# Storing the experts' results with an indexed GpSimd DMA that leaves empty places out, in a one-core decoder step

## The chip, the core and the metric

The kernel is one program on one core of a Trainium2 chip. The metric is the device time of one execution in microseconds, the median over the runs of the same kernel. A profiled execution gives the trace; its times count from the first instruction of the program, and its span ends with the last.

The engines are named as in the profile: PE (TensorE; PEld its weight loads), DVE (VectorE), ACT (ScalarE), POOL (GpSimd) and SP (SyncE, which only issues DMAs here). A q behind a name (POOLq, SPq) is that engine's sequencer, which issues and waits.

## The reference, cut to what matters

One layer of a decoder runs for 1024 prompt tokens and 64 sample tokens. After attention, a gated MLP and their merge, every token goes to two of 32 experts:

```
order = jnp.argsort(flat_e)
counts = jnp.zeros((N_EXPERTS,), jnp.int32).at[flat_e].add(1)
...
slot_tok = jnp.full((P,), T, jnp.int32).at[dest].set(flat_tok[order])
...
def run_block(args):
    xi, e = args
    return (jax.nn.silu(xi @ w_g[e]) * (xi @ w_u[e])) @ w_d[e]
yb = lax.map(run_block, (xb, block_e)).reshape(P, D)
out = jnp.zeros((T + 1, D), jnp.float32).at[slot_tok].add(yb.astype(jnp.float32) * slot_w[:, None])
```

So tokens are sorted by expert into blocks of 128 places, a block is run through its expert's three matrices (1024x512, 1024x512, 512x1024, fp32), and each token adds its two results, weighted. Places that no token fills have no part in the output. After that come a gate, a projection, norms and the output rows.

## The kernel before

The program is a row of stages, each a block in which all five engines run their own hand-written order; a stage ends with a barrier of all engines (in the trace each engine shows a DRAIN and an EVENT_SEMAPHORE there, on the line that opens the stage's block). Around the change they are: prompt attention (line 785), sample attention, merge, output projection, routing and experts in one block (line 2256), overflow (line 2449), and the final stage (line 2594).

**The experts.** The 32 experts are ranked by load. The 16 largest get a unit of 128 places each, the 16 smallest share 8 units, 64 places each: `NUNIT` is 24. Beyond them stand `NOVER` = 20 spare blocks for tokens of an expert that overflows its unit, so the table of results `c.y_d` (named moe_out) has `SLOTS` = 44 x 128 rows of 1024 floats, 4 KB a row. Per unit u, GpSimd gathers the token rows from moe_in in four indexed DMAs of a quarter row each (`gather_rows`), DVE lays them out (`lay_x`, which frees the gather's buffer and signals `xt_set`), PE makes gate, up and down products, DVE multiplies (`multiply`), and ACT copies the result out of PSUM into one of two buffers `Y` (`keep_y`, signal `y_done`) and stores all its 128 rows in moe_out with one DMA on its own queue, 512 KB. On PE the order is gate of u+1, down of u, up of u+1. SP streams the weights, 96 loads of 2 MB through nine slots, each issued when PE has left its slot.

**GpSimd's order in the experts' stage** is: the gathers of units 0 and 1, a small norm, then for u from 2 to 23 a wait for `xt_set` (u-1 units laid out) and the gather of u.

**The table's spare blocks** have to hold zeros or anything finite only where something reads them; they are cleared in the prompt attention. There GpSimd, in step with PE's gate products (semaphore `gate_mm`, one for each of 48 pieces), issues five DMAs of a 2 KB row of zeros repeated, 2 MB each. SP loads the gates' weights in the same stage, 1 MB for every two pieces, when `gate_mm` says that PE has begun the block before; the wait values 8q+6 of the clears are even, so that a clear is issued in the same microsecond or so as a load. PE needs that load when it comes to the first piece two pieces on (line 915).

**The end.** When the experts' block is left, the overflow stage loads the number of overflow blocks on each engine and steps over its loops (there is no overflow in these inputs), and the final stage begins: GpSimd waits for all stores of results and gathers two rows of moe_out per token, 128 tokens at a time (line 2622), while PE keeps itself busy with idle products (line 154), then turns the rows and makes the last gate products (lines 2674 and 2689).

The routing that the changed lines belong to runs on DVE as a chain of small operations, nearly each waiting for the one before (`do`, `tt`); `c.idx` holds for each place of a block the sum over its tokens of token number minus 4096, thus 0 where no token is. `block_at` is 128 times the block's number.

Of the kernel before, what the change touches and what calls it, by code (L numbers as in the profile page):

```python
# [15 lines left out]
I32 = mybir.dt.int32  # L16
U32 = mybir.dt.uint32
ALU = mybir.AluOpType
# [3 lines left out]
P = 128  # L22
D = 1024
# [16 lines left out]
PLE = 256  # L40
# [9 lines left out]
STRIPS = 4  # L50
SW = P // STRIPS
QW = D // STRIPS
NOWHERE = 4096
# [4 lines left out]
W_AT = HT_AT + TOK * KD  # L58
# [26 lines left out]
def bcast(ap, n):  # L85

    return ap.unsqueeze(2).to_broadcast([ap.shape[0], ap.shape[1], n])
# [43 lines left out]
def view(c, at, *dims):  # L131
    n = int(np.prod(dims))
    v = c.arena[:, at:at + n]
    if len(dims) == 1:
        return v
    names = "abcd"[:len(dims)]
    return v.rearrange(f"p ({' '.join(names)}) -> p {' '.join(names)}",
                       **{k: d for k, d in zip(names, dims)})
# [595 lines left out]
def stage_prompt_attention(nc, c):  # L734
# [50 lines left out]
    with nc.Block() as block:  # L785
        @block.sync
        def _(sp):
# [44 lines left out]
            c.load_keys(sp, 0, 2)  # L832
            sp.wait_ge(c.blank_out, 16 * BLANKS)

        @block.gpsimd
        def _(pool):
            pool.wait_ge(c.out_rows, 16 * 7)
            g_ = nc.gpsimd
            g_.memset(zeros, 0.0).then_inc(blank, 1)
            g_.memset(c.CN, 0.0).then_inc(c.cleared, 1)  # L840
            g_.memset(c.NOUGHT, 0.0).then_inc(c.cleared, 1)
            g_.memset(AT[:, NP], 0.0).then_inc(c.cleared, 1)
            pool.wait_ge(c.cn_in, 16 * H)
            for b in range(DB):
                g_.tensor_tensor(c.NBN[:, b, :], c.CN, c.new_mask[:, NS - b * DT:2 * NS - b * DT],
                                 ALU.add).then_inc(c.nbn_done, 1)
            pool.wait_ge(blank, 1)
            spare = c.y_d[NUNIT * P:].rearrange("(p n) (a d) -> p (n a) d", p=P, a=2)
            each = 2 * NOVER // BLANKS
            for q in range(BLANKS):  # L850
                pool.wait_ge(gate_mm, 8 * q + 6)
                pool.dma_start(spare[:, q * each:(q + 1) * each, :],
                               zeros.unsqueeze(1).to_broadcast([P, each, D // 2])).then_inc(c.blank_out, 16)
            pool.wait_ge(c.pages_in, 16)
            c.first_values = [c.page_numbers(pool, 0, ch) for ch in range(NCH)]
# [204 lines left out]
                    keep_out(m - 2)  # L1060


BLANKS = 5
CH = 4
NCH = PAGES // CH
NTI = P // 32
# [770 lines left out]
NUNIT = NSINGLE + NPAIRED  # L1837
GROUP = 5
NOVER = 20
SLOTS = (NUNIT + NOVER) * P  # L1840
HALF = P // 2
UNITS = []
# [6 lines left out]
LATE_AT = T_AT - 7 * WBLK  # L1849
# [63 lines left out]
def stage_route(nc, c):  # L1913
# [16 lines left out]
    iota, bonus, step_no, SEL, lane, block_at, tok, strip_no, step8 = route_tables(c)  # L1930
# [20 lines left out]
    xg_in = c.xg_in = [c.kept_sem(f"xg_in{j}") for j in range(2)]  # L1951
    c.g_strips = view(c, LATE_AT - NUNIT * STRIPS - QW, QW)
    c.quarter_i = view(c, LATE_AT - NUNIT * STRIPS, STRIPS, NUNIT).bitcast(I32)
    quarters_of_rows = c.h2_d.rearrange("t (s n) -> (t s) n", s=STRIPS)

    def gather_rows(g, u):
# [147 lines left out]
    def route_dve(dve):  # L2104
        v = nc.vector
# [11 lines left out]
        def tt(out, a, b, op):  # L2117
            do(v.tensor_tensor(out, a, b, op))
# [8 lines left out]

        dve.wait_ge(c.logit_mm, NT)
        dve.wait_ge(c.aux, NAUX)
        tt(LG, c.bank[6][:, 0:NT * K].rearrange("p (t k) -> p t k", k=K), bcast(c.stat[:, 2, :], K), ALU.mult)  # L2130
        tt(LG, LG, over_tiles(c.b_route[:], K), ALU.add)
        dve.sem_inc(logits_read, 1)
# [73 lines left out]
        for ch in range(NCHUNK):  # L2206
            if ch >= 2:
                dve.wait_ge(idx_mm, ch - 1)
            n = ch * LANES
# [8 lines left out]
                        strip_no, ALU.mult, ALU.add).then_inc(c.quarter_done, 1)  # L2218


        BY_RANK = GT
        tt(BY_RANK[0:1], lane[0:1, 0:NE].unsqueeze(2).to_broadcast([1, NE, NE]),
           rank[0:1].unsqueeze(1).to_broadcast([1, NE, NE]), ALU.is_equal)
# [14 lines left out]
def stage_moe(nc, c):  # L2238
# [4 lines left out]
    Y = view(c, MOE_AT + 6 * D, 2, D)  # L2243
# [4 lines left out]
    y_out = c.y_out = [c.kept_sem(f"y_out{j}") for j in range(2)]  # L2248
# [3 lines left out]
    down_mm, y_done = c.kept_sem("down_mm"), c.sem("y_done")  # L2252
# [3 lines left out]
    with nc.Block() as block:  # L2256
# [24 lines left out]
        @block.gpsimd  # L2281
        def _(pool):
            c.route["pool"](pool)
            g = nc.gpsimd
            for u in range(2, NUNIT):
                pool.wait_ge(xt_set, u - 1)
                c.gather_rows(g, u)

        @block.tensor
        def _(pe):  # L2290
# [63 lines left out]
        @block.scalar  # L2354
        def _(act):
            c.route["act"](act)
            s = nc.scalar

            def silu(u):
                act.wait_ge(gate_mm, u + 1)  # L2360
                if u >= 1:
                    act.wait_ge(act_done, CELLS * u)
                s.activation(SG, gate_ps[:, :], ACT.Silu).then_inc(silu_done, 1)  # L2363

            def keep_y(u):
                b = UNITS[u][0]
                act.wait_ge(down_mm, u + 1)
                if u >= 2:
                    act.wait_ge(y_out[u % 2], 16 * (u // 2))
                s.activation(Y[:, u % 2, :], y_ps, ACT.Copy).then_inc(y_done, 1)  # L2370
                act.wait_ge(y_done, u + 1)
                act.dma_start(c.y_d[b * P:(b + 1) * P, :], Y[:, u % 2, :]).then_inc(y_out[u % 2], 16)

            silu(0)
            for u in range(NUNIT):
                if u + 1 < NUNIT:
                    silu(u + 1)
                keep_y(u)
# [524 lines left out]
```

## Time and profile before

| | us |
|---|---|
| median of 3 runs | 1859.94 |
| lowest and highest run | 1856.11, 1860.59 |
| the profiled execution | 1858.34 |
| its span in the trace | 1856.7 |
| PE busy in the span | 1765.6 (95%) |
| DVE, ACT, POOL busy | 751.6, 317.8, 271.6 |
| DMA moved | 432.38 MB, mean 233 GB/s |

The span is 1.6 us shorter than the time of its execution. PE's busy time is the length of its work as the trace models it. What counts for a change is which wait ends last at its place: the page's shares are averages over stages, of which the prompt attention (344 to 706 us) leaves the DMA engines half idle and the experts' stage (1133 to 1700 us) keeps them busy throughout. "DMA share" in a row by windows is the mean busy share of the 16 DMA engines. Landing is the time from a DMA's issue to the semaphore that tells of its end.

### The profile page before, as it was taken

Reading aid. Unit: us, or ns where it says so; the run is one execution under the profiler, and the core shown is the slowest. Engines: PE = TensorE matmul, PEld = TensorE weight load, DVE = VectorE, ACT = ScalarE, POOL = GpSimd, SP = SyncE. Lnnn points to the kernel's source line nnn. Section 1 sums busy time; section 2 is a strip of 40 time slices with the busy share of each in tenths; the row PEclk is TensorE's granted clock in tenths of the full one; section 3 lists DMA queues with packets and bytes.
Section 4 is the critical chain, followed back from the end, with each engine's and each line's share of the span. In section 5 each row is a group of like instructions: output and inputs, shape, how many; then the busy total and the mean of one; then the engine's idle time right before and its main releaser. Section 6 shows DMA issues by size and latency. Waiting matters only on the chain. (4 is left out here: it accounts for less than half of the span.)

```text
span 1856.7 us, 23215 instructions
## 1 busy us (share of the span) xinstructions
PE 1765.6 (95%) x8503; PEld 894.0 (48%) x8503; DVE 751.6 (40%) x1539; ACT 317.8 (17%) x552; POOL 271.6 (15%) x390
## 2 busy tenths in 40 slices
PE   7999999899999998979999998999999999998997
PEld 4564554556566664544455444443333333433443
DVE  4201104433334354555322226444444444443665
ACT  2000001222222233322110113200000000000122
POOL 1000004200000002332300000421111122100330
PEclk9999999999999999999999999899999999998999
DMA  8012110344344638999747425699999999998541
GB/s 288 6 19 87 49 52 1 107 139 162 117 162 142 219 100 293 355 378 330 261 170 284 162 82 229 224 344 424 423 425 424 425 423 424 421 429 320 199 153 62
DMA packets 137027, 432.38 MB, mean 233 GB/s; under 512 B 26581, under 2 KB 65194, under 8 KB 124626
## 3 DMA queue, kind: packets, MB, share of 16 engines
q1 hardware_dynamic: 101026, 337.16, 47.7%
q0 software_dynamic: 20288, 62.98, 9.4%
q10 hardware_dynamic: 15600, 30.75, 4.4%
q8 instruction: 68, 1.11, 0.2%
q14 instruction: 45, 0.37, 0.1%
HBM read 378.99 MB, written 55.51 MB: 234 GB/s over the span
## 5 line engine op out<-in xcount | busy, mean ns | idle before, releaser
L2308 PE MATMUL psum<-arena 128*128 128x512 f32 (+1 forms) x1024 | 337.1, 595 | 0.0
L915 PE MATMUL psum<-arena 128*128 128x384 f32 (+1 forms) x768 | 253.9, 476 | 4.2 <-ACT arena L946 4.1
L2410 DVE TENSOR_TENSOR arena<-arena,psum 32x128 f32<-32x128 f32 x384 | 143.4, 373 | 267.2 <-PE psum L2308 256.0
L2308 PEld LDWEIGHTS psum<-arena 128*128 128x128 f32 (+1 forms) x1024 | 131.6, 163 | 203.0 <-issue 203.0
L2339 PE MATMUL psum<-arena 128*64 128x512 f32 (+1 forms) x512 | 170.4, 596 | 10.0 <-issue 6.0
L915 PEld LDWEIGHTS psum<-arena 128*128 128x128 f32 x768 | 139.8, 191 | 77.8 <-issue 6.0
L1959 POOL DMA_INDIRECT arena<-moe_in,arena x96 | 98.5, 1026 | 385.3 <-DVE arena L2392 322.4
L2339 PEld LDWEIGHTS psum<-arena 128*64 128x64 f32 (+1 forms) x512 | 68.5, 163 | 111.9 <-issue 111.9
L1764 PE MATMUL psum<-arena 128*128 128x512 f32 x256 | 114.7, 604 | 1.6 <-PEq L1539 1.6
L2689 PE MATMUL psum<-arena 128*128 128x512 f32 x256 | 111.4, 592 | 1.4 <-DVE arena L2721 1.4
L330 PE MATMUL psum<-arena 128*128 128x512 f32 x256 | 111.8, 593 | 0.7 <-DMA arena<-in_w_in 0.7
L1195 POOL DMA_DIRECT2D arena<-in_cache_v x112 | 60.1, 537 | 121.3 <-PE psum L1299 114.4
L1764 PEld LDWEIGHTS psum<-arena 128*128 128x128 f32 x256 | 48.2, 192 | 59.0 <-issue 59.0
L2689 PEld LDWEIGHTS psum<-arena 128*128 128x128 f32 x256 | 47.9, 190 | 58.5 <-issue 58.5
L1230 PE MATMUL psum<-arena 128*128 128x512 f32 x160 | 73.4, 601 | 2.6 <-DVE arena L1440 2.6
L330 PEld LDWEIGHTS psum<-arena 128*128 128x128 f32 x256 | 47.9, 190 | 57.9 <-issue 57.0
L953 ACT ACTIVATE arena<-arena 128x128 f32<-128x128 f32 (+7 forms) x64 | 49.1, 768 | 144.1 <-DVE arena L1017 80.4
L1426 DVE STREAM_TRANSPOSE arena<-arena 128x2048 f32<-128x2048 f32 x27 | 61.8, 2300 | 21.9 <-DMA arena<-in_cache_k 21.9
L2363 ACT ACTIVATE arena<-psum 128x512 f32<-128x512 f32 x24 | 14.3, 597 | 301.4 <-PE psum L2308 301.4
L390 PE MATMUL psum<-arena 128*128 128x384 f32 (+1 forms) x192 | 58.7, 469 | 1.6 <-DVE arena L536 1.6
L355 PE MATMUL psum<-arena 128*128 128x384 f32 (+1 forms) x192 | 58.8, 469 | 0.0
L644 PE MATMUL psum<-arena 128*128 128x512 f32 x128 | 56.8, 598 | 1.7 <-PEq L225 0.9
(298 smaller groups left out, 1846.6 us busy)
## 6 DMA issues: line engine op xcount, KB each, us to landing
arena<-in_w_exp_gate SPq DMA_DIRECT2D x32, 2048.0 KB, 22.1
arena<-in_w_exp_up SPq DMA_DIRECT2D x32, 2048.0 KB, 18.9
arena<-in_w_exp_down SPq DMA_DIRECT2D x32, 2048.0 KB, 21.4
arena<-in_cache_v POOLq DMA_DIRECT2D x128, 256.0 KB, 9.4
arena<-in_cache_k SPq DMA_DIRECT2D x124, 256.0 KB, 8.6
arena<-in_w_in SPq DMA_DIRECT2D x24, 1024.0 KB, 6.2
moe_out<-arena ACTq DMA_DIRECT2D x24, 512.0 KB, 10.4
arena<-in_w_in SPq DMA_DIRECT2D x5, 2048.0 KB, 20.1
```

The source lines that it names most:

```text
L330: last = mm(c.bank[4 + r % 3][:, :], hidden_tile(HT, t)[:, k, :], W[:, n + 1, k, :], start=(k == 0), stop=(k == KD - 1))
L355: last = mm(c.bank[n % 4][:, 0:CUTS[sec + 1] - CUTS[sec]], W[:, 0, k, j * P:(j + 1) * P], HT[sec][:, k, :], start=(k == 0), stop=(k == KD ...
L915: done = mm(c.bank[7][:, 0:b - a], WG[blk % 2][:, k, q * P:(q + 1) * P], HT[p // NCOL][:, k, :], start=(k == 0), stop=(k == KD - 1))
L1195: pool.dma_start(VC[:, ch, g, :], c.cache_v[bass.ds(numbers[ch][g] * P, P), :]).then_inc(v_in[ch], 16)
L1230: last = mm(c.bank[7][:, :], UP[col % 2][:, n, k, :], src[:, 4 * half:4 * half + 4, k, :], start=(k == 0), stop=(k == KF - 1))
L1426: v.transpose(keys, keys).then_inc(turned[b % 2], 1)
L1764: last = mm(c.bank[2 * (t % 2) + half][:, :], MT[:, k, t * P:(t + 1) * P], WO[:, k, half * 512:half * 512 + 512], start=(k == 0), stop=(k ...
L1959: g.indirect_dma_start(out=XG[:, u % 2, q, :], out_offset=None, in_=quarters_of_rows, in_offset=bass.IndirectOffsetOnAxis(ap=c.quarter_i[: ...
L2308: last = mm(out[rows_, :], XT[:, u % 2, k, rows_], c.ring_tile(LOAD[kind, u, r])[:, k, :], start=(k == 0), stop=(k == KD - 1))
L2339: last = mm(y_ps[rows_, cols], ACT_T[:, u % 2, k, rows_], c.ring_tile(LOAD["down", u, r])[:, k, cols], start=(k == 0), stop=(k == KF - 1))
L2410: v.tensor_tensor(ACT_T[SW * s:SW * s + SW, u % 2, :, SW * q:SW * q + SW], SG[r, cols].rearrange("p (d k) -> p k d", k=KF), up_ps[r, cols] ...
L2689: last = mm(gate_ps[t % 2][:, half * 512:half * 512 + 512], XT[:, t % 2, k, :], c.wpg[half][:, k, :], start=(k == 0), stop=(k == KD - 1))
```

## The change

Results are no longer stored by ACT. GpSimd stores unit u's 128 rows with an indexed DMA whose index per row is the place in moe_out, or `SLOTS` more than that where no token fills the place; a bounds check drops such rows. Since those rows of moe_out are then not written, the whole table is cleared in the prompt attention instead of its 20 spare blocks, in four DMAs instead of five. DVE works out the indices with one operation at the start of the routing and four at its end. GpSimd's order gets the store of unit u-3 behind the gather of u, and the last three stores follow the last gather.

```
-            spare = c.y_d[NUNIT * P:].rearrange("(p n) (a d) -> p (n a) d", p=P, a=2)
-            each = 2 * NOVER // BLANKS
+            spare = c.y_d.rearrange("(p n) (a d) -> p (n a) d", p=P, a=2)
+            each = 2 * SLOTS // P // BLANKS
...
-BLANKS = 5
+BLANKS = 4
...
+        place_in_block = c.stat[:, 3, 0:1]
+        do(v.tensor_scalar(place_in_block, tok[:, 0:1], float(NOWHERE), None, ALU.add))
...
+        do(v.tensor_scalar(row_f, c.idx[:, 0:NUNIT], 0.0, float(SLOTS), ALU.is_equal, ALU.mult))
+        tt(row_f, row_f, block_at[:, 0:NUNIT], ALU.add)
+        do(v.tensor_scalar(row_f, row_f, place_in_block, None, ALU.add))
+        v.tensor_copy(c.row_i, row_f).then_inc(c.rows_done, 1)
...
+            def scatter(u):
+                b = UNITS[u][0]
+                pool.wait_ge(y_done, u + 1)
+                g.indirect_dma_start(out=c.y_d, out_offset=bass.IndirectOffsetOnAxis(ap=c.row_i[:, b:b + 1], axis=0),
+                                     in_=Y[:, u % 2, :], in_offset=None,
+                                     bounds_check=SLOTS - 1, oob_is_err=False).then_inc(y_out[u % 2], 16)
+
+            pool.wait_ge(c.rows_done, 1)
             for u in range(2, NUNIT):
                 pool.wait_ge(xt_set, u - 1)
                 c.gather_rows(g, u)
+                if u >= 3:
+                    scatter(u - 3)
+            for u in range(NUNIT - 3, NUNIT):
+                scatter(u)
...
             def keep_y(u):
-                b = UNITS[u][0]
                 act.wait_ge(down_mm, u + 1)
                 if u >= 2:
                     act.wait_ge(y_out[u % 2], 16 * (u // 2))
                 s.activation(Y[:, u % 2, :], y_ps, ACT.Copy).then_inc(y_done, 1)
-                act.wait_ge(y_done, u + 1)
-                act.dma_start(c.y_d[b * P:(b + 1) * P, :], Y[:, u % 2, :]).then_inc(y_out[u % 2], 16)
```

GpSimd in the experts' stage, from the block's start to its end, in the kernel before; moe_in is where token rows are gathered from, and the last row but one leaves the block:

```order
L1634 UNCONDITIONAL_BRANCH
L2281 UNCONDITIONAL_BRANCH
L1959 DMA arena<-moe_in,arena 128x256 x8
L2008 TENSOR_SCALAR arena<-arena 128x9
L2010 TENSOR_TENSOR arena<-arena,neghalf 128x9
L1959 DMA arena<-moe_in,arena 128x256 x88
L2256 UNCONDITIONAL_BRANCH
L2467 UNCONDITIONAL_BRANCH
```

Every gather is done with when the block still has some 70 us to go. The end of the same list in the changed kernel, where line 1963 is the gather and 2300 the store:

```order
L1963 DMA arena<-moe_in,arena 128x256 x4
L2300 DMA moe_out<-arena 5632x1024
L1963 DMA arena<-moe_in,arena 128x256 x4
L2300 DMA moe_out<-arena 5632x1024
L1963 DMA arena<-moe_in,arena 128x256 x4
L2300 DMA moe_out<-arena 5632x1024 x4
L2267 UNCONDITIONAL_BRANCH
L2488 UNCONDITIONAL_BRANCH
```

A store stands between every two gathers, and four stores follow the last gather; the last of them waits for the last result of the stage and is GpSimd's last instruction in the block. ACT at the same end, in the kernel before (2370 copies a result out of PSUM, 2372 stores it):

```order
L2370 ACTIVATE arena<-psum 128x1024
L2372 DMA moe_out<-arena 128x1024
L2370 ACTIVATE arena<-psum 128x1024
L2372 DMA moe_out<-arena 128x1024
L2256 UNCONDITIONAL_BRANCH
```

In the changed kernel the copies stand alone, and the branch out of the block follows the last copy.

GpSimd in the prompt attention, the difference at the clears:

```order
 L845 TENSOR_TENSOR arena<-arena,new_mask 128x64 x8
-L852 DMA moe_out<-arena 128x8x512 x5
+L852 DMA moe_out<-arena 128x22x512 x4
 L1084 TENSOR_LOAD arena
```

The clears stand where they stood; each is 22 half rows a partition instead of 8, and the fifth is gone.

## Rows read from the trace of the kernel before

**Rows 1.** Waits of PE, 1195 to 1710 us: total, times, longest
```profile
PE psum L154 <- PEq L2449: 6.8, 1, 6.8
PE psum L2339 <- issue: 6.0, 15, 0.4
```
**Rows 2.** Windows: length, busy by engine (x count), PE clock, DMA share, GB/s
```profile
1400.00:1500.00 100.00, 98.36 (x292) 39.48 (x290) 42.22 (x84) 7.51 (x9) 19.95 (x20) 1.00 1.01 423
```
**Rows 3.** Waits of PE, 380 to 700 us
```profile
PE psum L915 <- ACT arena L946: 0.9, 3, 0.3
```
**Rows 4.** Timeline of POOL and of SPq: start, length, engine line
```profile
451.44 0.89 POOL L852 DMA_DIRECT2D moe_out<-arena  x1 [62.95 <-PE psum L915]
...
387.79 0.43 SPq L790 DMA_DIRECT2D arena<-in_w_in  x1
...
452.05 0.43 SPq L790 DMA_DIRECT2D arena<-in_w_in  x1
...
572.53 0.43 SPq L790 DMA_DIRECT2D arena<-in_w_in  x1
```
**Rows 5.** Landing of the gate weights' loads issued at 452.05 and 466.19
```profile
DMA to landing us min/median/max: 11.7/11.7/11.7
...
DMA to landing us min/median/max: 5.6/5.6/5.6
```
**Rows 6.** DMA queues in 454 to 458 us: packets, MB, share
```profile
q0 software_dynamic: 306, 1.25, 79.5%
q1 hardware_dynamic: 294, 0.30, 21.3%
```
**Rows 7.** Timeline of PE where it turns to the freshly loaded weights
```profile
404.27 2.75 PE L915 MATMUL psum<-arena 128*128 128x384 f32 x8
...
465.95 2.82 PE L915 MATMUL psum<-arena 128*128 128x384 f32 x8 [0.30 <-ACT arena L946]
...
589.01 2.32 PE L915 MATMUL psum<-arena 128*128 128x320 f32 x8
```
**Rows 8.** Timeline of DVE in the routing
```profile
1141.26 0.17 DVE L2150 TENSOR_SCALAR arena<-arena 128x9 f32<-128x9 f32 x1
...
1174.32 2.02 DVE L2392 TENSOR_TENSOR arena<-arena 128x1024 f32<-128x1024 f32 x1 [1.15 <-DMA arena<-moe_in,arena]
```
**Rows 9.** Timeline of POOL, ACT and DVE in the experts' loop
```profile
1292.93 1.00 POOL L1959 DMA_INDIRECT arena<-moe_in,arena  x1 [16.68 <-DVE arena L2392]
...
1297.50 1.02 ACT L2370 ACTIVATE arena<-psum 128x1024 f32<-128x1024 f32 x1 [6.93 <-PE psum L2339]
...
1332.99 2.00 DVE L2392 TENSOR_TENSOR arena<-arena 128x1024 f32<-128x1024 f32 x1
```
**Rows 10.** Landing of 22 of ACT's 24 stores, 1200 to 1690 us
```profile
DMA to landing us min/median/max: 8.9/10.5/11.1
```
**Rows 11.** Timeline of ACT and POOL: the last result, the last gather's last part
```profile
1698.74 1.02 ACT L2370 ACTIVATE arena<-psum 128x1024 f32<-128x1024 f32 x1 [7.27 <-PE psum L2339]
...
1618.80 0.99 POOL L1959 DMA_INDIRECT arena<-moe_in,arena  x1 [0.30 <-issue]
```
**Rows 12.** End of the experts' block, by its line: duration ns, start
```profile
L2256 POOLq EVENT_SEMAPHORE  x2: 17/17/17, 1700.4 to 1700.4; - x2
L2256 POOLq DRAIN  x1: 16844/16844/16844, 1616.2 to 1616.2; - x1
...
L2256 ACTq DRAIN  x1: 153/153/153, 1700.2 to 1700.2; - x1
```
**Rows 13.** End of the sample attention's block, by its line
```profile
L1161 POOLq DRAIN  x1: 14646/14646/14646, 909.4 to 909.4; - x1
```
**Rows 14.** Landing of POOL's last two loads before it (issued 908.8, 909.4)
```profile
DMA to landing us min/median/max: 12.4/12.9/13.4
```
**Rows 15.** Landing of the final stage's first gather (issued at 1706.2)
```profile
DMA to landing us min/median/max: 4.6/4.6/4.6
```
**Rows 16.** Timeline of PE at the start of the final stage
```profile
1705.51 11.69 PE L154 MATMUL psum<-before 128*128 128x512 f32 x20 [6.81 <-PEq L2449]
```

More of the change, by code:

```diff
@@ L1953, in stage_route @@
     c.quarter_i = view(c, LATE_AT - NUNIT * STRIPS, STRIPS, NUNIT).bitcast(I32)
+    row_at = LATE_AT - NUNIT * STRIPS - QW - NUNIT
+    assert row_at >= W_AT + 8 * D + (PLE // P) * D
+    row_f, c.row_i = view(c, row_at, NUNIT), view(c, row_at, NUNIT).bitcast(I32)
+    c.rows_done = c.kept_sem("rows_done")
     quarters_of_rows = c.h2_d.rearrange("t (s n) -> (t s) n", s=STRIPS)
```

## The prediction

> **What bounds the kernel now.** I read the waits of PE first, then the DMA share by windows, then the ends of the blocks. The reader is to see that PE is the bound at every place that the change touches but one. In the experts' loop PE's own waits are 6.0 us in 15 pieces, and the rest of the list is shorter [rows 1]. The DMA engines are busy throughout that loop, at 423 GB/s [rows 2], yet no wait of PE is put down to a weight load: the DMA keeps exactly the pace of PE. In the prompt attention PE waits 0.9 us in all [rows 3]. The one place where PE stands is the passage from the experts to the final stage, 6.8 us [rows 1, 16]: the last result is copied at 1698.74, the barrier opens at 1700.4 [rows 11, 12], and PE restarts at 1705.51. Whatever holds that barrier holds all engines.
>
> **Fewer rows stored.** 1088 tokens times 2 are 2176 filled places of 3072, so 896 rows of 4 KB, 3.67 MB, are no longer written. At 423 GB/s that is 8.7 us of DMA time [rows 2]. It is worth nothing where PE isn't waiting for a DMA; it only lets the weights land earlier. I take 0. If the DMA were the bound it would give the 8.7 us.
>
> **The store behind the gathers.** In the loop the gather of unit v+4 starts at 1292.93, when DVE has laid out v+2; v's result is copied at 1297.50 to 1298.5 [rows 9]. In the new order the store of v stands ahead of that gather and waits for the copy. So the gather starts at 1298.6 plus 1.3 for the store's own issue (one row of 1.0 and a gap of 0.3), 1299.9, that is 7.0 us later. Queued behind the waiting store are only gathers; who waits for them is DVE's layout at 1332.99. From the first part's issue to a DRAIN that outlasts a gather the trace has 18.1 us (1614.90 to 1633.0, the first part being 3.9 ahead of the row at 1618.80) [rows 11, 12]. Add the whole landing of a store ahead of it, 11.1 us at most [rows 10]: 1299.9 + 18.1 + 11.1 = 1329.1, still 3.9 us before DVE asks. Cost 0; and when this cover is gone, each unit would lose what the gather is late. The two buffers of results are reused after two units, some 43 us, against a landing of 11. ACT is freed of 24 issues, but waits for PE anyway.
>
> **Indices.** One small DVE operation is 0.17 us, 0.2 with its gap [rows 8]. The one at the head of the routing lies in the chain that PE waits for: 0.2 us. The four at the end take 0.8 us and fall in the 1.15 us in which DVE waits for the first gather [rows 8]: 0. GpSimd's wait for them stands ahead of the gather of unit 2, which starts 20 us later.
>
> **The clears.** A clear is issued at 451.44, a load of gate weights at 452.05 [rows 4]. That load landed after 11.7 us, one without a clear beside it after 5.6 [rows 5]. While both run, the queues take turns, 306 packets of the clear and 294 of the load in 4 us [rows 6]; 1.25 MB over 306 is 4 KB a packet, 0.30 over 294 is 1 KB. So the load's 1024 packets need 1024 / 73.5 = 13.9 us if the clear lasts as long. The old one had 512 packets and ended in the middle; the new one has 1408 (5.77 MB), so it does last. A landing has start and end beside the packets. By the share in [rows 6] 294 packets of the load occupy 21.3% of 4 us, 0.85, so its 1024 take at least 3.0 of the quiet load's 5.6, and up to 2.6 are left; gaps between packets make that less, I take 1.6. So the load lands 15.5 us after its issue, at 467.5, and PE, which turned to it at 465.95 [rows 7], waits 1.6. Counted from the 11.7 instead, the second 512 packets now take 7.0 us in turns where alone they took 1.5, which gives 17.2: PE then waits 3.3 there, and 0.7 each at the first and the fourth clear, where 15.5 is just in time (403.3 against 404.27, 588.0 against 589.01) [rows 4, 7] and the third has more room: 4.7. I take 1.5, near the first count, since the 4 us of [rows 6] hold only full turns and no quiet time; the bounds are 0.5 and 4.7. The far end is a clear that passes whole before the load: 2 MB cost 6.1 us, 5.77 MB then 16.8, so landing after 22.4, which is 5.9 + 8.5 + 5 + 5.9 = 25 us over the four. [rows 6] speak against it. The fifth clear's absence frees nobody. Sum for the clears: 1.5.
>
> **The last store, and the block's end.** This is the main term. Before, POOL had long been drained when the stage ended, and the barrier at 1700.4 came right behind ACT's short DRAIN of 153 ns [rows 12]: ACT's store was still under way. GpSimd's DRAINs are of another kind. At the experts' end it lasted 16.8 us, from 1616.2 to 1633.0, though the last DMA's issue was over at 1619.8 [rows 11, 12]. At the sample attention's end it lasted until 924.05 [rows 13], and the last DMA, issued at 909.4, landed 13.4 us later, at 922.8 [rows 14]. So it ended 1.2 us after that landing. For the gather, whose landing the trace doesn't give, a landing like the stores' 10.5 would be 1629.3 [rows 10], and the DRAIN ended 3.7 after it. I read: a DRAIN on GpSimd waits until its DMAs have landed, and then 1.2 to 3.7 us. The new last store goes out at 1699.85 behind the copy [rows 11]. Beside little other traffic an indexed DMA of the same 512 KB lands after 4.6 us [rows 15]: 1704.45. With 1.2, the row in which DVE was idle as it is here, the DRAIN ends at 1705.65 and the barrier opens at 1705.7 instead of 1700.4: 5.3 us. With 3.7 it is 7.8. Nothing covers it, since PE and all others stand at this barrier, and the walk over the overflow stage, the idle products and the first gather all follow it unchanged [rows 16]. What was late before, the products at line 154, is late by the same amount.
>
> The Trainium skill (DMA: Bandwidth & Descriptors, Anatomy of one DMA) gives a DMA issued by GpSimd as 2.0 us plus its bytes over 436 GB/s, an estimate of 3.2 us for this store. The measured landing of 4.6 us for the same size is longer and decides; by the page's figure the term would be 3.9 instead of 5.3, and the sum 5.6.
>
> **Sum.** 5.3 + 1.5 + 0.2 + 0 = 7.0 us. The profiled execution of 1858.34 becomes 1865.3; it lay 1.6 below the median of 1859.94, which becomes 1866.9, slower by 0.38%. With the bounds of the two terms, 5.3 to 7.8 and 0.5 to 4.7, it is 1865.9 to 1872.6, both upper ends at once being unlikely; a last unit of small experts with few filled rows could land 1 us sooner, 1864.9.
>
> **Rivals.** (a) *GpSimd's DRAIN waits only for descriptors.* Then its last issue of 1.0 us moves the barrier by 0.6 us, and the final stage's own wait for the store (1704.45) is over before its first gather at 1706.2. Sum 0.6 + 1.7 = 2.3: 1862.2, no measurable change. For it: other DRAINs take a fraction of a microsecond; against it: the two long ones. (b) *The DRAIN takes a fixed time behind the last DMA.* Both rows fit this nearly better: 14.2 us after the issue at 1618.80 and 14.6 after 909.4. Then the barrier opens at 1699.85 + 14.4 = 1714.2, 13.9 us late; with 1.7 more 1875.5. Against it only that I know no reason for such a wait. (c) *The clears pass whole, or the gathers come late*: 25 us and more in place of 1.5, some 1890, for the reasons above unlikely. (d) *The DMA is the hidden bound of the experts' loop*, the relief of 8.7 us is real, and (a) holds: 1859.94 - 8.7 + 2.3 = 1853.5, faster. It decides only if PE waits for weights, and [rows 1] have no such wait. (e) That the empty rows are written after all would change the DMA's work and not the time, since nothing hangs on it; the forecast stands in that case.
>
> The Trainium skill (SBUF — State Buffer, two separate sides) says that GpSimd cannot write DMA descriptors while DVE holds their shared port. By it a store issued during DVE's layout waits for that to end; at the last store DVE is idle, so it would add nothing to the main term.
>
> **How the numbers follow.** Chances: forecast 0.62, (a) 0.18, (b) 0.10, (c) 0.06, (d) 0.04. A measurement of this kernel can tell about 0.3%, 5.6 us, from no change; the line is 1865.5. The forecast's case stretches from 1864.9 to about 1871 and noise of the median carries some of it below the line; I put 0.47 above and 0.15 within. Slower: 0.47 + 0.10 + 0.06 = 0.63; same: 0.15 + 0.18 = 0.33; faster 0.04. The range is to take in the forecast and (a), with a microsecond or two of spread of the median: 1860.5 to 1872.0, leaving out (b), (c) and (d), 0.20.
>
> **What would show it.** In the changed kernel's trace: at the experts' block's end a DRAIN on POOLq that begins near 1700 and ends about 1706, the barrier just behind it, and ACT's DRAIN some 5 us before it; PE's wait at line 154 near 12 us instead of 6.8; a wait of PE on in_w_in near 466 of 1 to 2 us and none or little at the other clears; no wait of DVE on moe_in within the loop beyond the first two units. Rival (a) shows the barrier at 1701; (b) shows it at 1714; (c) shows long waits on in_w_in or moe_in; (d) shows an experts' loop with a shorter cycle. The forecast is wrong if the barrier moves by less than 4 us, or if PE's loop changes its pace at all.

## The result, and the profile after

Over 20 runs of each on the same chip the changed kernel has a median of 1861.64 us (1856.88 to 1869.28) and the kernel before 1855.66 (1850.06 to 1861.39). The ratio is 1.003, with a 95% interval of 1.0019 to 1.0041: slower by about 5.6 us (the two medians lie 6.0 us apart; the ratio is an estimate over all runs and not the quotient of the medians). Two further comparisons on other occasions gave 1.0019 [1.0009, 1.0029] and 1.0020 [1.0008, 1.0032], 3.5 and 3.7 us. The forecast was slower by 7.0 us, to 1866.9. So the sign held, and the time lies in the stated range, but the size did not hold. The absolute time came out 5.3 us below the forecast, and 4.3 us of that is luck of the start: the median of three runs from which the forecast counted (1859.94) stands that much above the median of twenty. The time also lies below 1865.5, the prediction's own line between slower and the same, and next to the 1862.2 of its rival (a), whose mechanism the trace refutes below.

The profiled execution took 1864.14 us, its span 1862.5. The first view is the waits of PE at the end of the experts' stage in the changed kernel (engine, line, what it waited for; total, times, longest), to be read against [rows 1]:

```profile
PE psum L154 <- PEq L2470: 10.3, 1, 10.3
PE psum L2710 <- DVE arena L2742: 1.4, 1, 1.4
PE psum L2363 <- ACT arena L2393: 1.2, 1, 1.2
PE psum L2363 <- DVE arena L2436: 0.4, 1, 0.4
```

The wait at line 154 was 6.8 us and is 10.3. The 1.4, the 1.2 and the 0.4 are in the kernel before too, word for word but for the line numbers. Over the whole loop, 1195 to 1710 us, PE's waits of the changed kernel are these:

```profile
PE psum L2363 <- issue: 6.0, 15, 0.4
PE psum L2363 <- DVE arena L2436: 2.8, 7, 0.4
PE psum L2363 <- ACT arena L2393: 1.2, 1, 1.2
```

The first row equals its counterpart in [rows 1] to the last digit: the loop's pace has not changed. The end of the experts' block by its line (duration in ns, then the start), the answer to [rows 12]:

```profile
L2267 POOLq EVENT_SEMAPHORE  x2: 17/17/17, 1706.6 to 1706.7; - x2
...
L2267 ACTq DRAIN  x1: 1052/1052/1052, 1701.0 to 1701.0; - x1
L2267 POOLq DRAIN  x1: 4002/4002/4002, 1702.6 to 1702.6; - x1
```

GpSimd's DRAIN starts behind its last store instead of 84 us before the end, it ends at 1706.6, and the barrier opens there. ACT's DRAIN of 1.05 us covers the last copy and is over at 1702.0, 4.6 us before the barrier. The timelines of ACT, POOL and PE at this place (start, length; in brackets the idle time before and its releaser), the answer to [rows 11, 16]:

```profile
1700.98 1.02 ACT L2393 ACTIVATE arena<-psum 128x1024 f32<-128x1024 f32 x1 [7.27 <-PE psum L2363]
...
1702.80 0.97 POOL L2300 DMA_INDIRECT moe_out<-arena  x1 [7.33 <-ACT arena L2393]
...
1711.20 1.19 PE L154 MATMUL psum<-before 128*128 128x512 f32 x1 [10.26 <-PEq L2470]
```

The last copy ends at 1702.00, the store is issued 0.80 later, and it landed after 3.2 us, at 1706.0:

```profile
DMA to landing us min/median/max: 3.2/3.2/3.2
```

The DRAIN ends 0.6 us behind that landing. So from the end of the last copy to the open barrier the changed kernel takes 0.8 + 3.2 + 0.6 = 4.6 to 4.7 us, where the kernel before took 0.67; from the barrier to PE's first product it takes 4.5, where the kernel before took 5.1. I call the whole, from the last copy's end to PE's first product at line 154, the **passage**: 5.75 us before, 9.20 after, so 3.45 more.

In the prompt attention PE has no wait on a weight load, as in [rows 3]:

```profile
PE psum L915 <- ACT arena L946: 0.9, 3, 0.3
PE psum L887 <- ACT arena L962: 0.3, 1, 0.3
```

In the experts' loop (timeline of POOL) the store stands ahead of the gathers as forecast, with the first gather at 1302.95 for a copy that ended at 1300.80:

```profile
1301.63 1.02 POOL L2300 DMA_INDIRECT moe_out<-arena  x1 [15.21 <-ACT arena L2393]
1302.95 1.02 POOL L1963 DMA_INDIRECT arena<-moe_in,arena  x1 [0.31 <-issue]
1304.28 1.01 POOL L1963 DMA_INDIRECT arena<-moe_in,arena  x1 [0.30 <-issue]
```

**A trap in comparing the two spans.** They differ by 5.8 us, and only 3.45 of it is the passage. Of the rest, 1.9 us lie ahead of the experts' stage. Windows of the merge and of the output projection (length, busy by engine, PE clock, DMA share, GB/s), first of the kernel before, then of the changed one:

```profile
928.00:987.00 59.00, 55.55 (x224) 36.37 (x224) 15.71 (x30) 7.96 (x5) 0.00 (x0) 1.00 0.36 134
987.00:1133.00 146.00, 139.77 (x522) 68.62 (x522) 36.40 (x66) 24.55 (x28) 8.81 (x30) 0.98 0.46 179
```
```profile
926.30:987.00 60.70, 57.25 (x224) 37.26 (x224) 15.79 (x30) 7.96 (x5) 0.00 (x0) 0.97 0.36 130
987.00:1135.00 148.00, 141.93 (x522) 69.75 (x522) 36.39 (x66) 24.55 (x28) 8.82 (x30) 0.96 0.46 176
```

The same 224 and 522 products take 1.7 and 2.2 us longer at a lower mean clock (1.00 and 0.98 against 0.97 and 0.96; it has two levels, 1.2 and 2.4 GHz, and the changed kernel's execution had 82.5 us at the lower one, the earlier one 65.5). Neither stage is touched by the change. In the thirteen traces of this study the experts' stage begins anywhere from 1127.1 (end_2mb) to 1136.4 (short_walk), and these two kernels are the same up to there. So single spans are not compared below; what is compared is the passage in a trace, and the ratio over many runs.

One stretch of a trace can be compared, since it starts behind all that varies there: from the end of the last copy to the program's last instruction. It is 156.9 us in the kernel before, and 160.5, 160.9 and 160.2 us in the three traces of the changed kernel, 3.3 to 3.9 us longer. So what the passage loses does reach the end of the program.

### The profile page after: what moved, and what is told of

It is laid out like the page before. It is cut to its first block and busy times, and to the rows that moved or that the text cites. A ratio compares the mean times of both kernels' runs of the same rounds, so it can differ in the third digit from the quotient of the medians.

```text
span 1862.5 us, 23244 instructions
## 1 busy us (share of the span) xinstructions
PE 1770.8 (95%) x8503; PEld 898.0 (48%) x8503; DVE 752.6 (40%) x1544; ACT 317.7 (17%) x552; POOL 300.4 (16%) x413
## 5 line engine op out<-in xcount | busy, mean ns | idle before, releaser
L1764 PE MATMUL psum<-arena 128*128 128x512 f32 x256 | 116.0, 610 | 1.6 <-PEq L1539 1.6
L2710 PE MATMUL psum<-arena 128*128 128x512 f32 x256 | 111.4, 593 | 1.4 <-DVE arena L2742 1.4
L330 PE MATMUL psum<-arena 128*128 128x512 f32 x256 | 112.0, 595 | 0.0
L2300 POOL DMA_INDIRECT moe_out<-arena x24 | 24.3, 1014 | 371.1 <-ACT arena L2393 371.1
L1230 PE MATMUL psum<-arena 128*128 128x512 f32 x160 | 73.4, 602 | 2.6 <-DVE arena L1440 2.6
## 6 DMA issues: line engine op xcount, KB each, us to landing
arena<-in_w_exp_up SPq DMA_DIRECT2D x32, 2048.0 KB, 18.1
arena<-in_w_exp_down SPq DMA_DIRECT2D x32, 2048.0 KB, 18.4
```

The costliest lines, as they stand in the source:

```text
L330: last = mm(c.bank[4 + r % 3][:, :], hidden_tile(HT, t)[:, k, :], W[:, n + 1, k, :], start=(k == 0), stop=(k == KD - 1))
L1230: last = mm(c.bank[7][:, :], UP[col % 2][:, n, k, :], src[:, 4 * half:4 * half + 4, k, :], start=(k == 0), stop=(k == KF - 1))
L1764: last = mm(c.bank[2 * (t % 2) + half][:, :], MT[:, k, t * P:(t + 1) * P], WO[:, k, half * 512:half * 512 + 512], start=(k == 0), stop=(k ...
L2710: last = mm(gate_ps[t % 2][:, half * 512:half * 512 + 512], XT[:, t % 2, k, :], c.wpg[half][:, k, :], start=(k == 0), stop=(k == KD - 1))
```

## The experiments

The theory after this profile: **the whole cost is GpSimd's late DRAIN, and the rest of the change is free.** Its rivals: the clears cost part of it; the loop pays something by the store ahead of the gathers; or it is not the landing that the DRAIN waits for. Ratios are to the kernel before on the same chip. In the table, c is the end of the last copy, "landing" that of GpSimd's last DMA from its issue, "tail" the time from the landing to the end of GpSimd's DRAIN, "walk" the time between the two barriers of the overflow stage (a barrier counted at its last row on POOLq). Landing and tail are left out where GpSimd's last DMA is long over.

| kernel | ratio, interval | c to barrier | landing | tail | walk | passage |
|---|---|---|---|---|---|---|
| before | 1 | 0.67 | | | 4.92 | 5.75 |
| changed | 1.0030 [1.0019, 1.0041] | 4.70 | 3.2 | 0.6 | 4.34 | 9.20 |
| changed_again | 1.0019 [1.0009, 1.0029] | 5.92 | 4.4 | 0.57 | 4.31 | 10.39 |
| changed_third | 1.0020 [1.0008, 1.0032] | 4.71 | 3.2 | 0.58 | 4.32 | 9.19 |
| last_by_act | 1.0013 [0.9998, 1.0027] | 1.06 | 7.9 | 0.54 | 4.69 | 5.91 |
| last_by_act_again | 0.9987 [0.9977, 0.9998] | 0.94 | 7.8 | 0.54 | 4.64 | 5.74 |
| clear_only | 1.0004 [0.9993, 1.0016] | 0.67 | | | 4.91 | 5.74 |
| all_rows | 1.0036 [1.0021, 1.0051] | 6.01 | 4.5 | 0.58 | 4.34 | 10.50 |
| plain_store | 1.0035 [1.0020, 1.0051] | 7.02 | 6.0 | 0.58 | 4.30 | 11.48 |
| end_small | 1.0048 [1.0034, 1.0062] | 9.01 | 4.3 | 4.3 | 4.27 | 13.44 |
| end_2mb | 1.0076 [1.0061, 1.0090] | 13.13 | 8.7 | 4.0 | 4.32 | 17.61 |
| short_walk | 0.9998 [0.9982, 1.0014] | 0.67 | | | 2.54 | 3.37 |
| last_two_short | 0.9988 [0.9977, 1.0000] | 0.68 | | | 2.45 | 3.28 |

**changed_again, changed_third.** The changed kernel, nothing edited.

> The changed kernel once more, so that the others of this call have it beside them on the same chip. Expected of both theories: 1.003 of the kernel before (1.002 to 1.004), the barrier at the experts' end about 4.7 us behind the end of the last result's copy, and PE's wait at line 154 near 10.3 us.

> The changed kernel, to stand beside the next two on the same chip. Expected: 1.002 to 1.003 of before, first idle product of the final stage 9 to 10.5 us behind the end of the last copy.

Both slower, by 0.19% and 0.20%. The passage is 4.6 and 3.4 us longer than before, the measured times 3.5 and 3.7. The store's landing was 3.2, 4.4 and 3.2 us, GpSimd's DRAIN 4.00, 5.22 and 4.01 us: with nothing edited, a landing 1.2 us longer made a DRAIN 1.2 us longer. Between issue and landing SP's queue, which loads ahead for the final stage, still moved 0.10, 0.20 and 0.07 MB beside the store. The store itself is smaller than the prediction took it: its queue shows 144 packets and 0.36 MB, which is 88 rows of 4 KB and 56 packets of 4 bytes; so 40 of its 128 places are empty (16 of the small packets are there without a dropped row too, as all_rows shows).

**last_by_act.** Only the last unit's rows are stored by ACT, as before the change; GpSimd's last store is then that of unit 22, issued some eight microseconds earlier. Every later wait for the stores is made to count ACT's too (not shown).

```
-            for u in range(NUNIT - 3, NUNIT):
+            for u in range(NUNIT - 3, NUNIT - 1):
                 scatter(u)
...
                 s.activation(Y[:, u % 2, :], y_ps, ACT.Copy).then_inc(y_done, 1)
+                if u == NUNIT - 1:
+                    b = UNITS[u][0]
+                    act.wait_ge(y_done, u + 1)
+                    act.dma_start(c.y_d[b * P:(b + 1) * P, :], Y[:, u % 2, :]).then_inc(c.y_last, 16)
```

> The changed kernel, but the last unit's 128 rows are stored whole by ACT, as before; the other 23 stay with GpSimd. Theory (the barrier waits for GpSimd's DRAIN, and that for the landing of its last DMA): the last store of GpSimd is now issued 8 us before the last copy, its DRAIN is over before ACT's, the barrier comes 0.7 us behind the last copy instead of 4.7, PE's wait at line 154 falls from 10.3 to 6.8 us, and the time is 3.5 us less than the changed kernel's, 1.001 of before. Rival (the index work or the full clear cost most of the 6 us): the passage may shorten, but the time stays near 1.003.

> The changed kernel with the last unit's rows stored by ACT, a second time, since the first left its ratio (1.0013) within both theories. Theory (the whole cost is the late barrier): the passage is 5.8 us as in the first trace, and the ratio 1.000 to 1.0005. Rival (some 2 us of the cost lie elsewhere): 1.001 to 1.002 again.

GpSimd's and ACT's DRAIN at the block's end of last_by_act:

```profile
L2268 POOLq EVENT_SEMAPHORE  x2: 17/17/17, 1697.1 to 1697.2; - x2
...
L2268 POOLq DRAIN  x1: 8650/8650/8650, 1688.4 to 1688.4; - x1
...
L2268 ACTq DRAIN  x1: 152/152/152, 1696.5 to 1696.5; - x1
```

GpSimd's DRAIN now spans 8.65 us, because its store needs 7.9 to land, but it ends at 1697.04, 0.9 us behind the last copy (1696.11), and the passage is back at 5.9 and 5.7 us. ACT's own store was issued at 1696.13 and landed 4.9 us later, at 1701.0, when the barrier had been open for 3.8 us: ACT's DRAIN of 152 ns waits for no landing. One store of 24 given back to ACT thus takes away the whole of the passage's growth, and everything else of the change is still in. From the last copy to the program's end these two traces have 156.9 us, as before the change. The ratios of the two occasions, 1.0013 and 0.9987, lie 0.26% apart for one and the same kernel, their intervals only touching. So one ratio with its interval promises more than it holds; half of that spread, 0.13%, is some 2.4 us. Their middle is 1.0000.

**clear_only.** The kernel before with the whole table cleared, in four DMAs; nothing else.

```
-            spare = c.y_d[NUNIT * P:].rearrange("(p n) (a d) -> p (n a) d", p=P, a=2)
-            each = 2 * NOVER // BLANKS
+            spare = c.y_d.rearrange("(p n) (a d) -> p (n a) d", p=P, a=2)
+            each = 2 * SLOTS // P // BLANKS
...
-BLANKS = 5
+BLANKS = 4
```

> The kernel before with one part of the change: the whole table of results is cleared, in four DMAs of 5.77 MB. Theory: in the trace of the changed kernel no wait of PE on the gate weights shows, so 1.000 of before, no wait on in_w_in, clears landing after 21 to 23 us. Rival (the clears cost part of the 6 us through PE or later stages): 1.001 to 1.002, with a wait of PE in the prompt attention.

1.0004, that is 0.7 us with an interval from -1.3 to 3.0, and PE's waits in the prompt attention are 0.9 and 0.3 us, as in the kernel before. The ratio alone would still allow the forecast's 1.5 us; it is the missing wait of PE that says that the clears cost nothing. Why, the changed kernel's trace tells. There the clears are issued at 385.70, 449.65, 508.70 and 570.11, each taking 1.35 to 1.46 us of POOL instead of 0.89 [rows 4], and the four loads beside them landed after 7.5, 10.8, 14.4 and 12.4 us, not after 15.5. The queues of the changed kernel in 452 to 454, 456 to 458 us and, around the third clear, 517 to 519 (packets, MB, share):

```profile
q1 hardware_dynamic: 333, 0.34, 83.5%
...
q0 software_dynamic: 162, 0.66, 80.5%
q1 hardware_dynamic: 161, 0.16, 22.9%
...
q0 software_dynamic: 162, 0.66, 80.5%
q1 hardware_dynamic: 162, 0.17, 23.3%
```

The turns are as [rows 6] gave them, packet by packet, 162 of the one to 162 of the other in 2 us. What the sum missed is when they begin. The clear's first packet stands at 454.5, 4.8 us after its issue; the old clear's at 453.3, 1.9 us after its own, before any packet of its load. In the changed kernel the load issued at 450.26 had by then passed some 500 of its 1024 packets alone. At the third clear the packets began after 3.0 us, the load had less of a start, and it landed after 14.4 us, near the 15.5 of the sum. That load was issued at 509.33 and landed at 523.7, and PE turned to it at 526.61.

The start varies, and its cause isn't known. The eight clears of 1408 packets in the changed kernel's trace and in clear_only's began 3.0 to 5.6 us after their issue; of the five of 512 packets in the kernel before four began after 1.8 to 1.9 us, but the first after 4.2.

**all_rows.** The changed kernel with indices that leave no row out.

```
-        do(v.tensor_scalar(row_f, c.idx[:, 0:NUNIT], 0.0, float(SLOTS), ALU.is_equal, ALU.mult))
+        do(v.tensor_scalar(row_f, c.idx[:, 0:NUNIT], 0.0, None, ALU.mult))
```

> The changed kernel, but the index leaves nothing out: empty places are written too (3072 rows instead of 2176). Theory (the rows left out are worth nothing in time, since PE never waits for a weight load): the same time as the changed kernel within 1 us, 1.002 of before; the weights' loads land after some 22 us again instead of 18; the very last store lands 0 to 1 us later, and the barrier with it. Rival (the DMA is a hidden bound and the relief is worth something): PE's cycle in the loop grows, some 8.7 us more in all.

**plain_store.** The changed kernel with GpSimd's stores in the same places but without indices, whole blocks of 128 rows.

```
-                g.indirect_dma_start(out=c.y_d, out_offset=bass.IndirectOffsetOnAxis(ap=c.row_i[:, b:b + 1], axis=0),
-                                     in_=Y[:, u % 2, :], in_offset=None,
-                                     bounds_check=SLOTS - 1, oob_is_err=False).then_inc(y_out[u % 2], 16)
+                pool.dma_start(c.y_d[b * P:(b + 1) * P, :], Y[:, u % 2, :]).then_inc(y_out[u % 2], 16)
```

> The changed kernel, but GpSimd stores each unit with a plain DMA of all 128 rows; the index is worked out and not used. It tells the indexed form from the plain one. Theory (DRAIN follows the landing, in 0.6 us): the last store lands after 4 to 5 us, the barrier comes 5 to 6 us behind the last copy, and the time is that of the changed kernel. Rival (behind a plain DMA of GpSimd the DRAIN takes 4.0 us more than the landing, as it did in the run with 2 MB at the end, behind an indexed store only 0.6): barrier 9 us behind the last copy, time 3.5 us above the changed kernel's.

1.0036 and 1.0035, 6.7 and 6.5 us slower; the passage grew by 4.75 and 5.7. The end of the block in plain_store:

```profile
L2267 POOLq EVENT_SEMAPHORE  x2: 17/17/17, 1707.8 to 1707.9; - x2
...
L2267 ACTq DRAIN  x1: 1052/1052/1052, 1699.8 to 1699.8; - x1
...
L2267 POOLq DRAIN  x1: 6624/6624/6624, 1701.1 to 1701.1; - x1
```

Neither the index nor the omission of rows makes the DRAIN wait: it is that the last DMA is GpSimd's. The plain store was issued sooner (0.30 us behind the copy instead of 0.80) and landed later, after 6.0 us against 4.5 for the same 128 rows in all_rows. But beside it SP's queue moved 0.73 MB, beside all_rows' store 0.33 and beside the changed kernel's 0.07 to 0.20. So whether the plain form is the slower one isn't shown; the landings rise with what SP still loads. The all_rows kernel writes 3.67 MB more than the changed one; whether leaving the rows out is worth anything by itself isn't separable: all_rows' ratio is above the changed kernel's three, and its interval overlaps all of theirs. Its last landing of 4.5 us is hardly longer than the changed kernel's 4.4. The expectation that the weights' loads would again need some 22 us with all rows written did not come true: their medians are 18.1 to 19.6 us.

**end_small, end_2mb.** The kernel before, all stores by ACT, with one additional DMA of GpSimd at the end of the block, into spare rows that nobody reads: 16 KB or 2 MB.

```
                 c.gather_rows(g, u)
+            pool.wait_ge(y_done, NUNIT)
+            pool.dma_start(c.y_d[NUNIT * P:NUNIT * P + P, 0:32], Y[:, 0, 0:32]).then_inc(c.end_out, 16)
```
```
                 c.gather_rows(g, u)
+            pool.wait_ge(y_done, NUNIT)
+            pool.dma_start(c.y_d[NUNIT * P:NUNIT * P + 4 * P, :].rearrange("(p n) d -> p n d", p=P), Y[:, 0, :].unsqueeze(1).to_broadcast([P, 4, D])).then_inc(c.end_out, 16)
```

> The kernel before, with one more DMA that GpSimd issues after the last result is copied: 16 KB into a spare block that nothing reads. Theory (0.6 us behind the landing): landing after about 2 us, barrier 2.7 to 3.5 us behind the last copy instead of 0.7, time 2 to 3 us more, 1.0013. Rival (4.0 us behind the landing of a plain DMA): barrier 6 to 7 us behind, time 5.5 us more, 1.003.

> The kernel before, with one more DMA that GpSimd issues after the last result is copied: 2 MB into spare rows of the table that nothing reads. It adds that work alone. Theory (DRAIN waits for the landing): the DMA lands after about 9.5 us, GpSimd's DRAIN ends 0.6 to 1.2 us later, the barrier comes 10.5 to 11.5 us behind the last copy instead of 0.7, the time is 10 us more, 1.0055. Rival (DRAIN lasts a fixed 4 us behind a DMA, whatever its size): barrier about 4.7 us behind the copy, time 3.5 to 4 us more, 1.002.

GpSimd's last DMA by its line, its landing, and the DRAIN behind it by the block's line (duration in ns, start), first in end_small, then in end_2mb:

```profile
L2290 POOL DMA_DIRECT2D moe_out<-arena x1: 594/594/594, 1696.9 to 1696.9; - x1
...
DMA to landing us min/median/max: 4.3/4.3/4.3
...
L2257 POOLq DRAIN  x1: 8616/8616/8616, 1696.9 to 1696.9; - x1
```
```profile
L2290 POOL DMA_DIRECT2D moe_out<-arena x1: 797/797/797, 1694.2 to 1694.2; - x1
...
DMA to landing us min/median/max: 8.7/8.7/8.7
...
L2257 POOLq DRAIN  x1: 12731/12731/12731, 1694.2 to 1694.2; - x1
```

The landing grew by 4.4 us from 16 KB to 2 MB, and the DRAIN by 4.1: the DRAIN follows the landing. That refutes both rivals of the prediction. By (a) the barrier should have opened a microsecond behind the copy, whatever the size; by (b) the DRAIN should have been 14 us long in each, and it was 8.6 and 12.7 here and 4.0 in the changed kernel. Nothing of the reference's work is changed in these two kernels, and 16 KB alone cost 8.9 us (1.0048), with 7.7 us of it in the passage. That is more than the changed kernel's 0.36 MB did, since the tail was 4.3 us here. Both expectations on record for end_small were too low: they put the landing near 2 us and the barrier at most 7 us behind the copy, and it was 9.0. From the last copy to the program's end the two traces have 164.2 and 168.0 us, against 156.9.

**short_walk, last_two_short.** The walk over the overflow stage, 20 spare blocks in groups of `GROUP`, each group's loop being stepped over by every engine. short_walk is the kernel before with one group; last_two_short is the changed kernel with one group, and with the last two units' rows stored by ACT.

```
-GROUP = 5
+GROUP = 20
```
```
-            for u in range(NUNIT - 3, NUNIT):
-                scatter(u)
+            scatter(NUNIT - 3)
...
+                if u >= NUNIT - 2:
+                    b = UNITS[u][0]
+                    act.wait_ge(y_done, u + 1)
+                    act.dma_start(c.y_d[b * P:(b + 1) * P, :], Y[:, u % 2, :]).then_inc(c.y_last, 16)
```

> The kernel before with the overflow stage's loops in one group of 20 blocks instead of four groups of 5. Without overflow every engine then steps over one group instead of four between the two barriers; where there is overflow it would run all 20 blocks. It asks whether a microsecond of this passage is a microsecond of the kernel. Theory: the stretch between the two barriers, 5.0 us, shrinks by 1.9 us (three turns of about 0.63 us on GpSimd), and the time with it, 0.999 of before. Rival (something else covers the passage, such as PE's idle products or the clock behind it): the stretch shrinks and the time stays at 1.000.

> The changed kernel with the last two units' rows stored by ACT, so that GpSimd's last DMA lands 15 us before the end, and with the overflow stage's loops in one group of 20 instead of four of 5. Theory: GpSimd's DRAIN is over before ACT's, the barrier 0.7 us behind the last copy, the first idle product 3.2 us behind it (5.6 in the kernel before), and the time 2.2 us below the kernel before, 0.9988, faster than both kernels. Rival (the passage is not worth its microseconds, or the store on GpSimd costs 2 us elsewhere): 1.000.

PE's wait at line 154, in short_walk and in last_two_short:

```profile
PE psum L154 <- PEq L2449: 4.4, 1, 4.4
```
```profile
PE psum L154 <- PEq L2474: 4.3, 1, 4.3
```

It fell by 2.4 and 2.5 us in the traces. The measured times moved by -0.4 us [-3.3, 2.6] and -2.2 us [-4.3, 0.0]: both hold the -2.4, but the first holds zero as well and the second ends there. In the traces the stretch from the last copy to the program's end did shrink, from 156.9 to 154.1 and 154.2 us. With an overflow, one group would run all 20 blocks where four could do with five, so this trades a rare case for the usual one.

**What was not tried.** The changed kernel with only the spare blocks cleared: places of moe_out that no store fills would stay unwritten. clear_only answers the same question from the other side.

**A version that beats both?** last_two_short and last_by_act_again stand at 0.9988 and 0.9987 of the kernel before, with intervals that end at 1.0000 and 0.9998, and below changed_third (1.0020) of the same chip. They beat the changed kernel. Against the kernel before they are at the edge of what these runs can tell, and the same kernel had given 1.0013 once.

## Why the prediction was right and wrong

**What bounds.** Right: PE's waits in the loop stayed at 6.0 us in 15 pieces, the DMA engines moved 421 GB/s in 1400 to 1500 us (423 before [rows 2]), and only the passage grew.

**The DRAIN.** Right in kind, and shown: GpSimd's DRAIN outlasts the landing of GpSimd's DMAs, and the barrier comes behind it (the three traces of the changed kernel, end_small, end_2mb), while ACT's doesn't (last_by_act). The term, 5.3 of the forecast's 7.0 us, was mis-sized. It was 5.3 for the barrier; measured are 4.0, 5.25 and 4.0 in three traces (c to barrier, less 0.67). In pieces: the store goes out 0.8 us behind the copy's end and not 0.1, so +0.7; it lands after 3.2 or 4.4 and not 4.6, so -1.4 or -0.2; the tail is 0.6 and not 1.2, so -0.6. The Trainium skill (DMA: Bandwidth & Descriptors, Anatomy of one DMA) gave 3.2 us for this landing by its figures; two of three traces have that value, the third has 4.4. But the 3.2 were worked out for 512 KB, and the store moved 0.36 MB, for which the page's sum is an estimate of 2.8; for all_rows' full 512 KB it is 3.2 against a measured 4.5, and end_small's 16 KB took 4.3 where it would be 2.0. So the agreement is in part chance. The tail was chance too: 1.2 us was chosen over 3.7 because DVE was idle in that row, and in end_small and end_2mb DVE is idle as well and the tails are 4.3 and 4.0.

**From the barrier to PE.** Wrong: it was said to be unchanged. With four groups in the overflow stage the walk between the two barriers was 4.3 us where GpSimd came last, and 4.6 to 4.9 where it didn't. So of the 4.0 to 5.25 PE saw 3.4 to 4.6, and its wait at line 154 became 10.3 us where the prediction's list of signs had about 12. Every late GpSimd in the table has this walk of 4.3; the cause isn't known, and no run tests it.

**The clears.** Wrong, 1.5 us forecast, and no wait of PE for it in any trace. The step that failed is that both queues take turns from the load's first packet on. The turns are there, but they start late: where a wait of 1.6 us was forecast, the load passed half of its packets alone and landed after 10.8 us, not 15.5. The trace of the kernel before had a hint of it: beside its first clear, which began 4.2 us after its issue, the load had some 400 packets of a start.

**Fewer rows, the store ahead of the gathers.** Right, 0 each, by PE's waits in the loop. In the loop the gathers' parts landed after 12.0 us in the median, 14.4 at most; the one whose first part left at 1302.95 was laid out at 1335.26, and DVE has no wait on moe_in there, of 0.1 us or more. The weights' loads landed sooner than before (medians in 1240 to 1640 us for gate, up and down: 17.4, 17.8 and 18.4 us against 22.2, 18.6 and 20.7), and PE did not ask for them sooner. That they land sooner because of the change isn't shown: clear_only, whose loop is the old one, has 18.7, 18.6 and 19.9. Nor does any run test what a store costs that is issued while DVE works: none of the changed kernel's 24 stores is issued while an operation of DVE runs.

**The small DVE operation** at the head of the routing, 0.2 us: not separable. From the experts' stage's start to its last copy's end the kernel before took 566.73 us, the changed one 567.03, and the other traces lie between 566.5 and 567.1.

**The sum.** 3.4 to 4.6 for the passage, nothing for the clears, at most 0.3 for the head: 3.4 to 4.9 us. The three ratios say 5.6, 3.5 and 3.7, in the mean 4.3. The forecast's 7.0 less 1.3 or 0.1 (the term's pieces), less 0.6 (the walk), less 1.5 (the clears) gives 3.6 to 4.8. So the steps that failed are the 1.5 us for the clears, the 5.3 us of the DRAIN's term (4.0, 5.25 and 4.0 measured) and the unchanged walk behind it. The rest of the distance to 1866.9 is the starting point: three runs, one of them at 1856.11, had a median 4.3 us above that of twenty.

**Still open.** Why the tail behind the landing is 0.5 to 0.6 us where GpSimd issues a store for every unit, with indices or without, but 3.9 to 4.3 us in end_small, in end_2mb and in clear_only (last part of the last gather issued at 1619.8 and landed 10.0 us later, DRAIN until 1633.8), and 1.2 at the sample attention's end [rows 13, 14]. It isn't the size, nor the index, nor the direction: end_small and plain_store are both plain stores. It isn't DVE either: DVE is busy for 3.6 of the 3.9 us behind that landing in clear_only, and idle in end_small and end_2mb. What these long ones share is that GpSimd had issued only gathers for some time. That is a pattern, not a cause.

## What to carry to other kernels

Before a DMA is moved to GpSimd, look where its last one stands: a DRAIN of GpSimd at a stage's end waits until it has landed, and all engines wait with it, whereas a store on ACT's queue may still be under way. If the stage's last result must be stored, leave that one store to another engine. And start a forecast of a few microseconds from enough runs, or from the ratio, as the start alone was off here by more than the effect.

## What the runs showed of the hardware that was not expected

- GpSimd's DRAIN behind a store of 16 KB was 8.6 us long: landing 4.3 beside ACT's store of 512 KB, tail 4.3. Small bytes at a stage's end aren't cheap.
- At the stage's end an indexed store of 88 rows by GpSimd landed after 3.2, 3.2 and 4.4 us, with 0.07, 0.10 and 0.20 MB of SP's loads beside it, and one of 128 rows after 4.5 with 0.33 MB. The plain one of 128 rows took 6.0 with 0.73 MB. Behind ACT's copy the indexed one was issued after 0.80 us, the plain one after 0.30.
- A row that the bounds check drops still shows in the queue as a packet of 4 bytes: 88 of 4 KB and 56 of 4 bytes in the changed kernel's last store, 128 and 16 in all_rows'.
- A clear of 1408 packets began to move 3.0 to 5.6 us after its issue, one of 512 packets after 1.8 to 1.9, but once after 4.2; its issue took 1.35 to 1.46 us of POOL instead of 0.89.
- The same program's stages ahead of the experts differed by up to 9 us from trace to trace: the experts began at 1127.1 us in end_2mb, with 25.8 us of PE's lower clock ahead of it, and at 1136.4 in short_walk, with 39.1.
